# A hybrid attention and convolution layer: hand-placed orders on four engines, rearranged

## The reference, cut to what matters

```python
h = rms_norm(x, norm_w)                    # x: 1024 tokens x 1024
q, kv_all, gates, nsa_z, cv_h, cv_b, cv_c, cv_z = split(h @ w_in)
q = rope(rms_norm(q))                      # 8 heads x 64, 2 groups
k_c = rope(rms_norm(compress_blocks(k_c))) # blocks of 32 tokens, stride 16
v_c = compress_blocks(v_c)                 # hid = silu(flat @ w1 + b1); hid @ w2
k_s, k_w = rope(rms_norm(k_s)), rope(rms_norm(k_w))
o = g0 * attend(q, k_c, v_c)   \
  + g1 * attend(q, k_s, v_s)   \
  + g2 * attend(q, k_w, v_w)               # c: compressed, s: selected, w: window of 512
o_nsa  = o * silu(nsa_z)
o_conv = cv_b * (conv3(cv_c * cv_h) + conv_b) * silu(cv_z)
out = x + concat(o_nsa, o_conv) @ w_out
```

## Time and profile before

| what | value |
|---|---|
| time, median of 3 runs | 677.98 us (677.61 to 678.36) |
| profiled execution, own time | 678.36 us |
| profiled execution, span from the first to the last instruction | 676.6 us |
| PE busy | 654.6 us, 97% of the span |
| DVE, ACT, POOL busy | 72%, 56%, 29% |
| granted TensorE clock | 1.0 of full speed throughout |
| chain that ended last | PE 81%, DVE 10%, ACT 4%, issue 4%, DMA 1% |

### The profile page before, as it was taken

How to read it: one execution, slowest core, us unless ns; L and a number is a source line. 1 busy time by engine, 2 the same in 40 slices (tenths; PEclk the granted TensorE clock), 3 DMA queues, 4 the chain that set the end, 5 groups by cost and what they waited for, 6 DMA issues and landing times.

```text
span 676.6 us, 10300 instructions
## 1 busy us (share of the span) xinstructions
PE 654.6 (97%) x3513; PEld 550.9 (81%) x3513; DVE 484.9 (72%) x1151; ACT 379.5 (56%) x883; POOL 197.0 (29%) x216
## 2 busy tenths in 40 slices
PE   8999999999999999999989999899899999999998
PEld 5889998878887888888777888788678788887776
DVE  4945989984756555776687876878877768777753
ACT  6744458554435354466555674657875556655641
POOL 3423204523423232431222312123842221212120
PEclk9999999999999999999999999999999999999999
DMA  8423202211111111100101101011411001001111
GB/s 316 140 55 111 63 1 63 63 32 47 50 45 32 47 32 32 48 18 30 32 16 32 32 17 31 1 63 55 162 35 60 34 32 63 32 32 38 57 32 63
DMA packets 19636, 36.30 MB, mean 54 GB/s; under 512 B 2816, under 2 KB 4224, under 8 KB 19584
## 3 DMA queue, kind: packets, MB, share of 16 engines
q1 hardware_dynamic: 19440, 35.63, 16.9%
q10 hardware_dynamic: 144, 0.00, 0.0%
HBM read 31.43 MB, written 4.19 MB: 53 GB/s over the span
## 4 chain that ended last, share of the span: by engine, by line
PE 81%; DVE 10%; ACT 4%; issue 4%; DMA 1%; SPq 0%; POOL 0%; ACTq 0%; DVEq 0%
PE pf L1398 10%; PE pf L1399 9%; PE pf L1400 9%; PE tp L1691 7%; PE sc L1536 4%; PE pj L1400 4%; PE pj L1399 4%; PE pj L1398 4%; PE sc L1535 4%; PE po L1671 4%; PE po L1672 4%; PE sc L1398 3%; PE sc L1400 3%; PE sc L1399 3%; DVE ptl L1332 1%
## 5 line engine op out<-in xcount | busy, mean ns | idle before, releaser
L904 ACT CAST pth<-tp 128x512 fp32r<-128x512 f32 (+1 forms) x148 | 86.8, 586 | 119.8 <-PE tp L1691 118.6
L1310 DVE CUSTOM_DVE_ANT_0 sc<-sc,maskb 128x64 f32<-128x64 f32 (+8 forms) x192 | 103.2, 561 | 49.9 <-PE sc L1536 49.3
L1332 DVE TENSOR_TENSOR ptl<-tp,pth 128x512 fp32r<-128x512 f32 x132 | 91.1, 690 | 39.1 <-ACT pth L904 38.5
L627 POOL TENSOR_SCALAR qp<-qp,precip,gate 128x64 f32<-128x64 f32 x64 | 44.4, 694 | 175.4 <-DVE precip L1300 175.2
L1691 PE MATMUL tp<-cst,qp 128*128 128x128 f32 (+1 forms) x592 | 88.9, 272 | 2.4 <-issue 1.3
L1398 PE MATMUL pf<-hh,fh 128*128 128x512 f32 x200 | 80.6, 403 | 2.7 <-DVE mixc L1269 1.9
L1691 PEld LDWEIGHTS tp<-cst,qp 128*128 128x128 f32 (+1 forms) x592 | 68.8, 137 | 12.3 <-issue 3.4
L1399 PE MATMUL pf<-hl,fh 128*128 128x512 f32 x200 | 78.3, 392 | 0.0
L1400 PE MATMUL pf<-hh,fl 128*128 128x512 f32 x200 | 78.2, 391 | 0.0
L587 POOL TENSOR_TENSOR fl<-fraw,fh 128x512 fp32r<-128x512 f32 x36 | 48.7, 1354 | 92.7 <-ACT fh L753 92.7
L578 POOL TENSOR_TENSOR wl<-qp,wh 128x512 fp32r<-128x512 f32 (+1 forms) x33 | 49.3, 1519 | 88.8 <-ACT wh L667 85.2
(11 more groups left out here) (243 smaller groups left out, 1548.5 us busy)
## 6 DMA issues: line engine op xcount, KB each, us to landing
fraw<-in_wside SPq DMA_DIRECT2D x36, 256.0 KB, 2.6
qp<-in_wpack SPq DMA_DIRECT2D x28, 256.0 KB, 3.1
wor<-in_wout SPq DMA_DIRECT2D x16, 256.0 KB, 2.8
xo<-in_x SPq DMA_DIRECT2D x16, 256.0 KB, 2.8
out<-xo SPq DMA_DIRECT2D x16, 256.0 KB, 2.1
mixc<-in_xcm SPq DMA_DIRECT2D x4, 512.0 KB, 7.2
xlow<-in_xcm SPq DMA_DIRECT2D x3, 512.0 KB, 6.4
qp<-in_wpack SPq DMA_DIRECT2D x5, 224.0 KB, 2.6
```

The costliest lines, as they stand in the source:

```text
L904: nc.scalar.copy(pth[ptn % 2][0:r, :], tp[tpn % 2][0:r, :]).then_inc(pth_ready, 1)
L1310: return V.tensor_tensor_reduce(row, row, mask, -1.0, -NEG, ALU.add, ALU.min, most)
L1332: V.tensor_tensor(ptl[ptn % 2][:, :], tp[tpn % 2][:, :], pth[ptn % 2][:, :].bitcast(F32), ALU.subtract).then_inc(tp_read, 1)
```

## The change

On ACT, DVE and PE the transposes of the window keys and of the compressed keys are moved ahead among the gate tiles. The `inv_std` of the window keys moves from ahead of `block_lo(0)` into `normalise_k`, and `item(E_KC, 2)` moves ahead of `block_lo(0)` on DVE. For kind "c", ACT makes two copies in place of one (rows 0 to 63 and rows 64 to 127), and DVE's low part is made in place on the second. `queries` on ACT moves to the end of a step's list. On PE, at steps without a turn, `flush` moves ahead of the first two parts of side work. The diff in full:

```diff
--- before.py
+++ after.py
@@ -838,16 +838,16 @@
             nc.scalar.copy(ckr[:, 0, :], cmp_bank[0]).then_inc(ck_raw, 1)
             act.wait_ge(ck_sum, 1)
             root(S_CK, 1, HD, ck_std)
+            keys_hi(0, 4, 1)
             item(E_Z, 1)
+            keys_hi(2, 4, 1)
             item(E_Z, 2)
-            keys_hi(0, 4, 1)
             hidden(1)
-            keys_hi(2, 4, 1)
+            act.wait_ge(kt_done, 9)
+            nc.scalar.copy(kend[:, :, P:P + CB], xt[0][:, 0:P].rearrange("p (g c) -> p g c", g=GROUPS)).then_inc(kt_hi, 1)
             for h in range(2):
                 half_hi(h)
             item(E_Z, 3)
-            act.wait_ge(kt_done, 9)
-            nc.scalar.copy(kend[:, :, P:P + CB], xt[0][:, 0:P].rearrange("p (g c) -> p g c", g=GROUPS)).then_inc(kt_hi, 1)
             act.wait_ge(cmp_done, 2)
             for g in range(GROUPS):
                 for r in (0, CB):
@@ -900,8 +900,11 @@
                 act.wait_ge(tp_done, tpn + 1)
                 if ptn >= 2:
                     act.wait_ge(pv_done, ptn - 1)
-                r = CB if kind == "c" else P
-                nc.scalar.copy(pth[ptn % 2][0:r, :], tp[tpn % 2][0:r, :]).then_inc(pth_ready, 1)
+                if kind == "c":
+                    nc.scalar.copy(pth[ptn % 2][0:CB, :], tp[tpn % 2][0:CB, :])
+                    nc.scalar.copy(pth[ptn % 2][CB:P, :], tp[tpn % 2][0:CB, :]).then_inc(pth_ready, 1)
+                else:
+                    nc.scalar.copy(pth[ptn % 2][:, :], tp[tpn % 2][:, :]).then_inc(pth_ready, 1)
                 tpn += 1
                 ptn += 1
 
@@ -935,8 +938,6 @@
                         side(f)
                 for h in halves_at(k):
                     half_hi(h)
-                if queries_at(k) is not None:
-                    queries(queries_at(k))
                 for j in wout_at(k):
                     kt, cols = wout_piece(j)
                     act.wait_ge(wor_in[j % 4], 16 * (j // 4 + 1))
@@ -962,6 +963,8 @@
                     else:
                         act.wait_ge(mixc_used, m)
                     nc.scalar.copy(msh[:, 4:8, :], mixc[:, :, m * P:(m + 1) * P]).then_inc(msh_ready, 1)
+                if queries_at(k) is not None:
+                    queries(queries_at(k))
 
 
         @block.vector
@@ -1133,6 +1136,7 @@
 
             def normalise_k(idx):
 
+                inv_std(S_KV + 16 * idx, 16, HD, head_std, 1 + 2 * idx)
                 s = stat[:, 2, S_KV + 16 * idx:S_KV + 16 * idx + 16].rearrange("p (t h) -> p t h", t=NT)
                 krow = krows[idx]
                 v = krow[:, :, :, 0, :]
@@ -1191,7 +1195,6 @@
                 V.scalar_tensor_tensor(hdl, hid[:, 2], 0.5, hdh.bitcast(F32), ALU.mult, ALU.subtract)\
                     .then_inc(hdl_ready, 1)
 
-            inv_std(S_KV, 16, HD, head_std, 1)
             normalise_k(0)
             for m in range(NT):
                 item(E_KV1, m)
@@ -1207,9 +1210,8 @@
             positions(0)
             keys_lo(2, 0, 0)
             rotate_q(0)
-            inv_std(S_KV + 16, 16, HD, head_std, 3)
+            item(E_KC, 2)
             block_lo(0)
-            item(E_KC, 2)
             item(E_KC, 3)
             positions(1)
             hidden(0)
@@ -1218,21 +1220,21 @@
             block_lo(1)
             dve.wait_ge(ck_raw, 2)
             V.tensor_reduce(stat[:, 0, S_CK:S_CK + 1], cksq[:, :], AX.X, ALU.add).then_inc(ck_sum, 1)
+            keys_lo(0, 4, 1)
             inv_std(S_CK, 1, HD, ck_std, 1)
             c = ckr[:, 0, :]
             link(V.scalar_tensor_tensor(c, c, stat[:, 2, S_CK:S_CK + 1], hnorm[:, 1, :], ALU.mult, ALU.mult))
             link(rope(c, cst[:, C_COSC:C_COSC + ROT], cst[:, C_SINC:C_SINC + ROT], [cktmp[:, k, :] for k in range(4)]))
             V.tensor_copy(ckr[:, 1, :], c).then_inc(keys_normed, 1)
             item(E_Z, 1)
+            keys_lo(2, 4, 1)
             item(E_Z, 2)
-            keys_lo(0, 4, 1)
             hidden(1)
-            keys_lo(2, 4, 1)
-            item(E_Z, 3)
             dve.wait_ge(kt_hi, 9)
             low = kend[HD:P, :, P:P + CB]
             V.tensor_tensor(low, xt[0][HD:P, 0:P].rearrange("p (g c) -> p g c", g=GROUPS), low.bitcast(F32),
                             ALU.subtract).then_inc(kt_ready, 1)
+            item(E_Z, 3)
             dve.wait_ge(cv_hi, 1)
             for g in range(GROUPS):
                 for r in (0, CB):
@@ -1326,8 +1328,8 @@
                 nonlocal tpn, ptn
                 dve.wait_ge(pth_ready, ptn + 1)
                 if kind == "c":
-                    V.tensor_tensor(pth[ptn % 2][CB:P, :], tp[tpn % 2][0:CB, :], pth[ptn % 2][0:CB, :].bitcast(F32),
-                                    ALU.subtract).then_inc(tp_read, 1)
+                    low = pth[ptn % 2][CB:P, :]
+                    V.tensor_tensor(low, tp[tpn % 2][0:CB, :], low.bitcast(F32), ALU.subtract).then_inc(tp_read, 1)
                 else:
                     V.tensor_tensor(ptl[ptn % 2][:, :], tp[tpn % 2][:, :], pth[ptn % 2][:, :].bitcast(F32),
                                     ALU.subtract).then_inc(tp_read, 1)
@@ -1628,14 +1630,14 @@
             item(E_Z, 0)
             compressed(0)
             item(E_Z, 1)
+            key_transposes(0, 2, 4, 2)
             item(E_Z, 2)
-            key_transposes(0, 2, 4, 2)
+            key_transposes(2, 4, 4, 2)
             hidden(E_W1, 1)
-            key_transposes(2, 4, 4, 2)
-            item(E_Z, 3)
             pe.wait_ge(keys_normed, 3)
             pe.wait_ge(kt_ready, 7)
             nc.tensor.transpose(xt[0][:, 0:P], ckr[:, :, :].rearrange("p u d -> p (u d)"), ident).then_inc(kt_done, 1)
+            item(E_Z, 3)
             compressed(1)
 
             pe.wait_ge(ck_raw, 2)
@@ -1704,11 +1706,9 @@
                     if n % 2 == 1:
                         pe.wait_ge(cmp_scaled, 4 * (n // 2 + 1))
                     turn(n, *turned[0])
-                for p in side_parts(k, 0)[:0 if turned else 2]:
-                    channels(p) if p < OUT_0 else output(p)
-                if not turned:
+                else:
                     flush()
-                for p in side_parts(k, 0)[0 if turned else 2:]:
+                for p in side_parts(k, 0):
                     channels(p) if p < OUT_0 else output(p)
                 for t in turned[1:]:
                     turn(n, *t)
```

## The result

The changed kernel takes **683.92 us** (median of 5 runs, 683.16 to 685.11); the kernel before, on the same chip, takes 678.36 us (5 runs, 677.61 to 678.85). The medians differ by 5.6 us. The ratio is 1.0078, 95% interval 1.0065 to 1.0090, which is 5.3 us (4.4 to 6.1): it agrees with the mean of all 15 executions of the changed kernel on record (683.5 us; 682.41 to 685.11, median 683.33). The forecast was slower by 2.6 us at 681.0; the median of the five lies 0.1 us beyond the upper end of the stated range, that of the 15 inside it. The profiled execution took 683.84 us, its span is 682.0 us.

The account below looks back on a forecast made before the run. PE, busy 97% of the span, was taken as the bound. Terms 1.5 + 1.75 - 0.8 + 1.66 - 1.15 = +2.96 us on 677.98 gave 680.9, predicted as 681.0 us, 8 in 10 range 678.6 to 683.8.

Parts of the forecast that it names:

- Handover: From projections to attention: PE waits for window keys until about 141.45; +1.5 us, bounds +0.3 to +2.6.
- copies: Second ACT copy at 16 "c" tiles, showing where PE's cover is too short; +1.75 us, bounds nothing to +5.2.
- last flush: Step 133: PE reaches the flush early, stands still, six output projection matmuls come behind; +1.66 us, +1.1 to +1.8.
- queries: Queries behind ACT's copies: 0.7 us back at step 102, 0.45 at 118, 0 at 86; -1.15 us, -1.9 to +0.4.
- early flushes: Flush ahead of side work at 13 of 14 steps, helping behind steps 13 and 29; -0.8 us, -1.1 to +0.3.
- the named tiles: "c" tiles near 401, 532, 600 and 636 us, where the added copy shows: 0.52, 0.23, 0.56 and 0.43 us.
- the other eleven: Remaining "c" tiles before the last, costed at nothing: 0.6 us or more of cover, or DVE late for another reason.
- The rival with every late tile in full: Each late "c" tile pays its copy in full, 5.2 in place of 1.75 us: 684.4 us; chance 0.08.
- Small costs: Rival: copies hidden after all, keys come at 140.27 (+0.3): 677.4 us, or 678.4 with handover at +1.3; chance 0.14.
- The faster case: Rival: ACT's backlog near step 86 clears, exponentials done before 475.4, copies taken in: -1.8 us, 676.2; chance 0.08.
- The rival by the port rule: Handover: two-SBUF-input DVE instructions each queue behind a POOL piece, 3.8 us extra wait: 684.6 us; chance 0.03.
- a sign of being wrong: Prediction wrong if waits between steps 84 and 92 change by over 1 us in sum, or keys meet no wait.

Follow-up runs that it names:

- the filler: Changed kernel plus 13 throwaway matmuls of zeros on PE between the second gate tile and the window-key transposes: 682.14 us, ratio 1.0064.
- the kernel with the late last flush: Changed kernel with the flush of step 133 alone back behind its first six matmuls of output projection: 682.18 us, ratio 1.0068.

## Why the prediction was right in direction and too small

**The parts.** Handover 3.3, copies 3.4, last flush 1.4, 13 flushes -0.85, queries -1.6: 5.65 us, against 5.6 measured. Each experiment is good to 0.6 to 0.9 us (half a ratio's interval, 0.0009 to 0.0013, of 678), and the handover and the last flush are differences of two of them, so the sum is good to about 2 us and its fit to 0.1 us is luck; by the ratios it comes to 4.7 us against 5.3. The copies and the early flushes do interact, by the 0.3 us behind step 13.

**Handover: +1.5 predicted, 3.3 measured.** The mechanism was right: no wait for L1037, one of 3.15 us (2.5 to 3.5 was named) ended by L1149. The wait itself is 3.15 - 1.38 = 1.77 us dearer, near the term and inside its bounds. By the time of the earlier trace rows the keys came at 141.81, 0.36 us later than the 141.45 foreseen. That is not the scales, which took 1.13 us to the forecast's 1.18, but `hidden(0)` ahead of them, which took 0.4 us more beside POOL than before. The step that failed is the sentence "The clock is at its full level all through, so no term comes from it." It was read from the kernel before, whose longest wait here is 1.38 us, and carried over to one whose wait is over twice that. The clock fell to the 1.2 GHz level behind the wait and cost 1.6 us in the traced execution; the filler takes it back. This put 3.3 beyond the term's upper end of 2.6.

**Copies: +1.75 predicted, 3.4 measured.** A mis-sized term with the right mechanism. At the named tiles the loss was 2.4 us in place of 1.74; near 637 us, for one, the wait for the output rows grew from 0.38 to 0.90 us, not by 0.43. The larger miss is "the other eleven have 0.6 us or more, or DVE comes late for another reason": 1.1 us came there. Around steps 84 to 87, where ACT runs nearly without a gap, an added 0.58 us is not taken up by cover at PE but handed along ACT's list to the next low part (0.89 to 1.41 us), and there again the clock can fall behind the longer wait. The sum of idle time of ACT, 44%, said nothing of this place. The rival with every late tile in full (+5.2) was too dear.

**Last flush: +1.66 predicted, 1.4 measured** in the trace, with the wait of 1.51 us where 1.7 was named. **Early flushes: -0.8 predicted, -0.85 measured**; alone they bring the wait behind step 13 to 0.32 us, as foreseen, and remove the one behind step 29. **Queries: -1.15 predicted, -1.6 measured**: steps 102 and 118 as worked out; step 86, taken as 0, gave 0.3.

**What of the rivals.** Small costs failed on the covers of 0.06 us, which were real. The faster case failed where its own test said, at the exponentials of step 86; the waits between steps 84 and 92 changed by 0.8 us in sum (2.97 to 2.18), under the 1 us that was named as a sign of being wrong. The rival by the port rule had the contention right and its price wrong: the three instructions with two inputs each took about 1.1 us more, 3.2 us in all, but its condition, that none of the later ones be spared for it, did not hold, and the keys came 1.13 us later for the scales, not 3.8. An addition of 1.6 us was due there from the clock, which no rival named. That the total still came out near the top of the range is luck in part: the handover went beyond its own bounds, and the room it took had been left for other terms.

What stays open: what decides whether the clock falls near 480 us. Five traced kernels have the same two waits there, 1.41 to 1.43 and 0.58 or 0.59 us; it fell in one, the changed kernel, at a price of 0.5 to 0.6 us against the other four.

## What to carry to other kernels

An edit that gathers PE's waiting into one long wait can cost more than the wait: here, behind 3.15 us, PE worked at half clock for a while, so price a new wait of this length with the granted clock in mind, not only with the clock row of the kernel before. When PE must wait that long, matmuls of zeros into a free bank kept the clock. It is better to ask whether PE's order has to move at all: here copying earlier on ACT and DVE alone removed the old wait, and no other took its place there. Before comparing the times of events in two traces, find by how much one runs ahead of the other: the keys' 141.04 us looks earlier than the 141.45 foreseen, and with the 0.77 us by which that execution runs ahead it is later. An engine's idle share over the span says nothing of a stretch in which its list has no gap: work added there is late for whoever comes next.

## What the runs showed of the hardware

- A wait of PE of 3.15 us was followed by a stretch at the 1.2 GHz level: the three rows of the change fall short of 1.00 by (0.31 + 0.50 + 0.04) x 2 us = 1.7 us of full clock, which is 3.4 us at half clock. In the profiled execution of the kernel with the late last flush the same wait, 3.17 us until 142.03, had a longer one, of 6.8 us by the same sum (0.49, 0.50, 0.50 and 0.22 lacking from 141 to 149), and attention began about 1.2 us later than the later start of that execution explains. The same wait therefore has no one price: 1.6 us on top of it in the change, some 2.8 there (an estimate, 1.6 + 1.2). Two of the stretches of that kernel:

```profile
145.00:147.00 2.00, 2.00 (x6) 1.53 (x5) 1.38 (x2) 0.59 (x2) 0.00 (x0) 0.50 0.00 0
147.00:149.00 2.00, 2.00 (x8) 1.59 (x8) 1.69 (x5) 1.97 (x4) 0.00 (x0) 0.78 0.00 0
```

- Waits of 1.38 us alone and of 1.07 us left the clock at 1.00. Two waits with 1.1 us of work between them, 1.41 and 0.91 us, or 0.89 and 1.11, were followed by 0.50 in the traced executions; 0.89 and 1.42 were not, and 1.4 and 0.6 us were in one traced execution of five. Of the 19 executions of the kernel before on one chip, three had a mean clock of 0.997.
- Matmuls of zeros kept the clock at 1.00 in the traced executions, 13 of them over 3 us and 4 over 1 us. With the 13, four of five executions had a mean clock of 1.0, where all 15 of the changed kernel had 0.994 to 0.997.
- DVE instructions of 128x16 with two inputs took 1.22 to 1.32 us beside POOL's subtractions, one of which takes 1.26 us, and 0.17 or 0.18 us without them.
